# Last norm of a sparse-attention and expert layer: two tiles scaled by ScalarE and weighted by GpSimd, one expert choice summed by VectorE

## What is computed

```
proj = x @ W_in                      # q, k, v, indexer, pooling channels
mix  = concat(sparse attention with the top 128 keys, multi-scale pooling) @ W_out
h    = LayerNorm(alpha * x + mix) * ln1_g + ln1_b
# 4 groups x 8 experts; top-1 group, then top-2 experts c = 0, 1 in it, weights w[t, c]
ffn  = sum_c w[t, c] * (silu(h @ w_gate[e_c]) * (h @ w_up[e_c])) @ w_down[e_c]
out  = LayerNorm(alpha * h + ffn) * ln2_g + ln2_b
```

## Time and profile before

| | |
|---|---|
| median of 3 runs | 545.08 us (544.93 to 546.55) |
| the profiled execution | 548.01 us, its span 546.3 us |
| PE busy | 473.6 us, 87% |
| DVE busy | 227.7 us, 42% |
| ACT busy | 148.7 us, 27% |
| POOL busy | 170.3 us, 31% |
| DMA | 148.04 MB, mean 271 GB/s |
| granted TensorE clock, mean | 0.93 |

### The profile page before, as it was taken

The page is one execution under the profiler, slowest core; times in us unless marked ns, Lnnn a source line. Parts: engine busy times, 40 slices in busy tenths (PEclk is TensorE's granted clock), DMA queues, the critical chain, the costliest instruction groups (busy, mean ns, idle before and its releaser), DMA issues.

```text
span 546.3 us, 6192 instructions
## 1 busy us (share of the span) xinstructions
PE 473.6 (87%) x2210; PEld 274.2 (50%) x2210; DVE 227.7 (42%) x561; ACT 148.7 (27%) x313; POOL 170.3 (31%) x159
## 2 busy tenths in 40 slices
PE   4999999999988998996659999999877789757992
PEld 3587867687744566885624333343333333322341
DVE  2101899999856653538811112121101110101297
ACT  3323433361484673213401111021011110011032
POOL 3153599883354860333420111111111110100000
PEclk9999999999996999998559999899888998979898
DMA  9944469004088004984977999999999999999813
GB/s 313 356 61 51 51 91 390 20 1 154 1 281 297 0 1 125 427 334 175 363 260 304 398 421 421 418 420 421 419 418 422 420 421 418 422 420 386 328 54 154
DMA packets 42440, 148.04 MB, mean 271 GB/s; under 512 B 11284, under 2 KB 15892, under 8 KB 30120
## 3 DMA queue, kind: packets, MB, share of 16 engines
q1 hardware_dynamic: 37992, 139.71, 67.9%
q0 software_dynamic: 4320, 7.82, 3.9%
q10 hardware_dynamic: 96, 0.08, 0.0%
HBM read 137.16 MB, written 18.35 MB: 285 GB/s over the span
## 4 chain that ended last, share of the span: by engine, by line
PE 31%; DVE 25%; DMA 20%; SPq 15%; issue 4%; ACT 3%; POOL 2%; DVEq 0%; ACTq 0%; POOLq 0%
DMA wgu<-in_w_up_dram 10%; PE bank L1499 10%; SPq L497 10%; PE bank L1305 7%; DVE score L946 6%; DVE m L945 5%; DMA xe<-h_rows,row_from 5%; SPq L500 5%; DMA x_again<-in_x_dram 4%; DVE score L963 4%; PE bank L1523 3%; PE bank L1485 2%; PE bank L1348 2%; PE bank L1379 1%; PE bank L1587 1%
## 5 line engine op out<-in xcount | busy, mean ns | idle before, releaser
L1499 PE MATMUL bank<-wgu,xeT 128*64 128x512 f32 x512 | 128.8, 661 | 28.0 <-DMA wgu<-in_w_up_dram 27.1
L1499 PEld LDWEIGHTS bank<-wgu,xeT 128*64 128x64 f32 x512 | 42.9, 151 | 103.5 <-issue 102.4
L1128 DVE TENSOR_TENSOR act_row<-bank,sil 128x256 f32<-128x256 f32 x16 | 6.8, 424 | 152.9 <-ACT sil L857 152.9
L713 POOL DMA_INDIRECT y_rows<-ye,row_to x14 | 14.1, 1008 | 177.9 <-PE bank L1485 117.5
L1523 PE MATMUL bank<-wd,actT 128*64 128x512 f32 x256 | 57.9, 593 | 0.7 <-ACT actT L864 0.7
L620 POOL TENSOR_TENSOR ring_low<-ring,wt_high 128x1024 fp32r<-128x1024 f32 x16 | 38.7, 2416 | 42.9 <-ACT wt_high L740 42.2
L857 ACT ACTIVATE sil<-bank 128x256 f32<-128x256 f32 x16 | 6.1, 383 | 153.7 <-PE bank L1499 153.7
L1523 PEld LDWEIGHTS bank<-wd,actT 128*64 128x64 f32 x256 | 19.7, 137 | 35.6 <-issue 35.6
L1305 PE MATMUL bank<-xT_high,wt_high 128*128 128x512 f32 (+1 forms) x136 | 35.6, 406 | 0.0
L1305 PE MATMUL bank<-xT_low,wt_high 128*128 128x512 f32 (+1 forms) x136 | 35.2, 402 | 0.0
L678 POOL TENSOR_SCALAR lg<-lg,rinv 128x128 f32<-128x128 f32 (+3 forms) x32 | 22.2, 693 | 38.5 <-DVE rinv L1024 38.4
(11 more groups left out here) (199 smaller groups left out, 700.7 us busy)
## 6 DMA issues: line engine op xcount, KB each, us to landing
wgu<-in_w_gate_dram SPq DMA_DIRECT2D x32, 1024.0 KB, 21.7
wgu<-in_w_up_dram SPq DMA_DIRECT2D x32, 1024.0 KB, 26.6
wd<-in_w_down_dram SPq DMA_DIRECT2D x32, 1024.0 KB, 28.7
ring<-in_w_in_dram SPq DMA_DIRECT2D x5, 2048.0 KB, 17.2
wo<-in_w_out_dram SPq DMA_DIRECT2D x2, 2048.0 KB, 7.9
y_rows<-zero SPq DMA_DIRECT2D x1, 4096.0 KB, 21.4
yg<-y_rows SPq DMA_DIRECT2D x8, 512.0 KB, 8.7
bias_rows<-brow SPq DMA_DIRECT2D x1, 2560.0 KB
```

The lines of the kernel that those rows point to most:

```text
L1499: ins = pe.matmul(bank[2 + i][half_rows(n), :], xeT[i][:, k, half_rows(n)], wgu[slots[n]][:, :, k, :], start=k == 0, stop=k == KD - 1)
```

## The change

For tiles 0 and 1 (`BY_POOL = 2`) the normalised rows are made by other engines. VectorE's `shift(t)` forms the reciprocal of the deviation and -mean/std, two one-column instructions (L1247, L1248 of the changed kernel). ScalarE makes yg[t][0] = h * (1/std) - mean/std, one pass (L933). GpSimd multiplies it by g2 and adds b2, two passes (L736, L737), and SP waits for GpSimd's semaphore before the stores of these tiles. Tiles 2 and 3 are centred and finished by VectorE as before, the centring in a function of its own.

TensorE's `stored_rows(3)` takes only the first choice of tile 3 (two products in place of four, one diagonal matrix in place of two); VectorE adds the second with `add_stored(3, 1)`. VectorE's stored passes are split by choice and placed between the last sums.

```diff
@@ SP
             for t in range(NT):
-                sp.wait_ge(out_ready, t + 1)
+                if t < BY_POOL:
+                    sp.wait_ge(out_pool_ready, t + 1)
+                else:
+                    sp.wait_ge(out_ready, t - BY_POOL + 1)
                 sp.dma_start(ov[t], yg[t][1][:, :]).then_inc(out_stored, 16)
@@ GpSimd, behind its last store of rows
+            pool.wait_ge(ln2_in, 32)
+            for t in range(BY_POOL):
+                pool.wait_ge(norm2_ready, t + 1)
+                link(pool.tensor_tensor(yg[t][0][:, :], yg[t][0][:, :], g2[:, :], ALU.mult))
+                pool.tensor_tensor(yg[t][1][:, :], yg[t][0][:, :], b2[:, :], ALU.add).then_inc(out_pool_ready, 1)
@@ ScalarE, in the loop over tiles, behind the Sqrt
+                if t < BY_POOL:
+                    act.wait_ge(shift2_ready, t + 1)
+                    act.activation(yg[t][0][:, :], h[:, t, :], ACT.Identity, bias=row_sum[:, t, 0:1], scale=rstd2[:, t:t + 1]).then_inc(norm2_ready, 1)
@@ VectorE
-                    for c in range(2):
-                        ins = dve.tensor_scalar(by_weight[:, c, :], ident[:, :], wt[:, NT - 1, c:c + 1], None, ALU.mult)
-                    ins.then_inc(by_weight_ready, 1)
+                    dve.tensor_scalar(by_weight[:, :], ident[:, :], wt[:, NT - 1, 0:1], None, ALU.mult).then_inc(by_weight_ready, 1)
...
+            def shift(t):
+
+                dve.wait_ge(std2_ready, t + 1)
+                link(dve.reciprocal(rstd2[:, t:t + 1], std2[:, t:t + 1]))
+                dve.tensor_scalar(row_sum[:, t, 0:1], neg_mean[:, t:t + 1], rstd2[:, t:t + 1], None, ALU.mult).then_inc(shift2_ready, 1)
...
             gated(LAST)
-            add_stored(0)
-            add_stored(1)
+            for t in range(2):
+                for c in range(2):
+                    add_stored(t, c)
             y_out(LAST)
-            add_stored(2)
+            add_stored(2, 0)
+            add_last(0)
+            add_stored(2, 1)
+            add_last(1)
+            shift(0)
             dve.wait_ge(ln2_in, 32)
-            add_last(0)
-            for t in range(1, NT):
-                add_last(t)
-                finish(t - 1)
-            finish(NT - 1)
+            add_last(2)
+            centre(2)
+            shift(1)
+            add_stored(3, 1)
+            add_last(3)
+            centre(3)
+            finish(2)
+            finish(3)
@@ TensorE, stored_rows
-                    for c in range(2):
-                        pe.matmul(bank[LAST_BANKS[t][i]][:, :], by_weight[:, c, :], yg[t][c][:, 512 * i:512 * i + 512], start=c == 0, stop=False)
+                    pe.matmul(bank[LAST_BANKS[t][i]][:, :], by_weight[:, :], yg[t][0][:, 512 * i:512 * i + 512], start=True, stop=False)
```

More of the change, by code:

```diff
@@ L64 @@
 PLACE = 4
+BY_POOL = 2
 PAIR_SLOTS = ((2, 3), (1, 0), (4, 5))
@@ L176, in layer_kernel @@
         place_w = at("place_w", o + 10 * KB, [NT, 2, CAP])
-        by_weight = at("by_weight", o + 10 * KB, [2, P])
+        by_weight = at("by_weight", o + 10 * KB, [P])
         sil = [at(f"sil{i}", o + 4 * KB + KB * i, [DE]) for i in range(2)]
@@ L333, in layer_kernel @@
         std2_ready = sem("std2_ready")
+        shift2_ready = sem("shift2_ready")
+        norm2_ready = sem("norm2_ready")
+        out_pool_ready = sem("out_pool_ready")
         h_ready = sem("h_ready")
@@ L1210, in _, with add_stored @@
                         ins.then_inc(o_added, 1)
-            def add_stored(t):
+            def add_stored(t, c):
                 dve.wait_ge(y_gathered[t], 32)
-                for c in range(2):
-                    link(dve.scalar_tensor_tensor(out=h[:, t, :], in0=yg[t][c][:, :], scalar=wt[:, t, c:c + 1], in1=h[:, t, :],
-                                                  op0=ALU.mult, op1=ALU.add))
+                link(dve.scalar_tensor_tensor(out=h[:, t, :], in0=yg[t][c][:, :], scalar=wt[:, t, c:c + 1], in1=h[:, t, :],
+                                              op0=ALU.mult, op1=ALU.add))
             def add_last(t):
@@ L1225, in add_last, with centre @@
                 dve.sem_inc(mean_ready, 1)
+            def centre(t):
                 link(dve.scalar_tensor_tensor(out=yg[t][0][:, :], in0=h[:, t, :], scalar=neg_mean[:, t:t + 1], in1=g2[:, :],
                                               op0=ALU.add, op1=ALU.mult))
+            def shift(t):
+                dve.wait_ge(std2_ready, t + 1)
+                link(dve.reciprocal(rstd2[:, t:t + 1], std2[:, t:t + 1]))
+                dve.tensor_scalar(row_sum[:, t, 0:1], neg_mean[:, t:t + 1], rstd2[:, t:t + 1], None, ALU.mult).then_inc(shift2_ready, 1)
             def finish(t):
```

## The result

The changed kernel took 548.45 us (median of 15 runs, 546.58 to 550.49), the one before 545.45 (15 runs, 542.84 to 550.50). The medians differ by 3.0 us. The ratio is 1.0048 with a 95% interval of 1.0026 to 1.0070, which is slower by 2.6 us, with 1.4 to 3.8 inside the interval. The forecast was 2.5 slower, 547.6 us.

What follows compares the result with a forecast made beforehand. VectorE's last pass plus 3.1 us was taken to set the end; passes alternating with GpSimd's, 14.99 us from 530.73, end it 2.49 us later: 545.08 + 2.5 = 547.6 us. Forecast's own range 546.6 to 549; stated range 545.3 to 549.0.

Steps and rivals of the forecast that it cites:

- VectorE sets the end, the last pass plus 3.1 us: Tail: VectorE has no gap longer than about 0.1 us; the end is its last pass plus 3.1 us.
- GpSimd starts at 530.7: Tail: GpSimd's first pass on tile 0 follows ScalarE's scaling, at 530.7 us, possibly 0.2 earlier or 1.0 later.
- Alternation: Tail behind 530.7: four GpSimd passes and VectorE's five two-input SBUF passes take turns, 14.99 us to the last finish.
- held passes: Tail: VectorE's passes waiting on GpSimd; centre of tile 2 about 3.0 us, second choice of tile 3 2.9, finish 2 3.1.
- release steps: Tail: a waiting VectorE pass ends 1.10 us after its release, a waiting GpSimd pass 2.27.
- TensorE's removed work is worth nothing by itself: Last tiles' banks: TensorE loses two products, 1.7 us less, worth nothing alone because VectorE was the later of the two.
- VectorE's removed passes: Tail: VectorE loses four passes of 1.30 us, gains one and two small scalar products; net 3.4 us less.
- A product by a pointer scalar is free beside GpSimd: Tail: VectorE's two new scalar products with a pointer operand, 0.21 us each, are not held by GpSimd.
- rival 3: Tail: tile 1's shift on VectorE also waits for GpSimd's second pass; +3.0, 548.1 us; chance 10%.
- Rival 1: Tail: engines run side by side, but stores queue at about 1.25 us each; -0.3, 544.8 us, no change; chance 15%.
- Rival 2: Tail: engines run side by side and the three stores overlap, each landing 2.6 us after issue; 543.3 us, faster; chance 7%.

Runs made afterwards that it cites:

- e3: The change, but VectorE centres and finishes all four tiles, with GpSimd and ScalarE's scaling out; 547.62 us, 1.0016 of the kernel before.
- e7: The change, but TensorE sums the second choice of tile 3 again and VectorE's pass for it is out; 546.61 us, 1.0014 of the kernel before.
- e1: The change without GpSimd's four passes over tiles 0 and 1, eight columns cleared in their place; 543.13 us, 0.9944 of the kernel before.
- e2: The change with GpSimd's two passes per tile replaced by five memsets that read nothing; 546.98 us, 1.0002 of the kernel before.
- e4: The change, but ScalarE copies g2 and b2 into emptied banks, where VectorE's centre and finish read them; 546.03 us, 0.9990 of the kernel before.
- e6: As e4, but SP stores the tiles in the order 0, 2, 3, 1; 544.70 us, 0.9972 of the kernel before.

## Why the prediction was right

The mechanism was right, and so was its size. That 2.5 and 2.6 us agree to 0.1 is partly luck: the interval is far wider, and the small errors below have both signs.

1. *VectorE sets the end, the last pass plus 3.1 us.* The change ends 3.20 behind its last pass (546.1 - 542.90), e3 3.08, before 3.07. So of the 2.46 us that the tail grew, 2.33 are the last pass, where 2.49 were forecast.
2. *GpSimd starts at 530.7*, which is 24.2 us behind the first gate/up product; it was 24.37. The first sum came at 17.43 against 17.23: counted back from the end of 16 records the first bank came out 0.2 us too early. The second sum, which waits for its own bank, was 0.09 late (18.29 against 18.20), and about as much again was lost between ScalarE's end and GpSimd's start, 0.15 us (528.08 to 528.23) where the forecast had less than 0.1.
3. *Alternation.* Forecast of the held passes: 3.0, 2.9, 1.5, 3.1 us; measured 3.12, 2.93, 1.43, 3.05. The release steps were set at 1.10 and 2.27 and are 1.08 and 2.21, so the sum from GpSimd's start to the last finish was 14.67 us against 14.99. That more than cancels the late start: last finish forecast at 39.2, measured 39.04.
4. *TensorE's removed work is worth nothing by itself.* e3 and e7 show it: the 1.7 us of TensorE came with a pass of VectorE that costs 0.95 in the change and 1.74 without GpSimd. VectorE's removed passes are worth 2.83 us to its last finish where GpSimd doesn't hold the rest (e1, 36.71 - 33.88); in the change the holds took more than that.
5. *A product by a pointer scalar is free beside GpSimd* (against rival 3): L1248 of tile 1, issued at 531.89 while GpSimd's pass ran from 531.66 to 533.87, took 0.21. The prediction took rival 3 for the rule of the Trainium skill (SBUF — State Buffer, Who interferes with whom). That section says only that a tensor_scalar can enter a two-port mode, when its operands meet conditions; it doesn't say that a product over one column does, and this one was not held.
6. Rival 1 was nearly right in size where its premise is made true: without exclusion VectorE ends 2.8 us earlier than before (e1) and the queue of stores takes that back (e2, e4). From GpSimd's last pass to the end of the span e4 took 40.43 - 34.77 = 5.66 us, against 3.07 behind VectorE's last pass before, where one store is left: 1.3 us for each of the two stores more, where the rival had 1.25. Rival 2's unqueued stores did not occur.

That the second engine to come waits for the whole of the other's pass is shown by the chain of ends and by e1, e2 and e4. Which part of the memory's ports it is, no run here can tell.

## What to carry to other kernels

Work moved from VectorE to GpSimd is only off VectorE if the passes left to VectorE have at most one input in SBUF (e4), or if GpSimd's instruction reads nothing from SBUF (e2). One input on GpSimd's side is enough for exclusion, as the kernel before shows. Its L655 on GpSimd reads one tensor of SBUF, its L963 on VectorE two (timelines of before):

```profile
107.73 0.98 DVE L963 SCALAR_TENSOR_TENSOR score<-relu,iw,score 128x512 f32<-128x512 f32 x1
108.12 1.06 POOL L655 TENSOR_SCALAR_AFFINE_SELECT bias<-bias 128x512 f32<-128x512 f32 x1
108.74 0.98 DVE L963 SCALAR_TENSOR_TENSOR score<-relu,iw,score 128x512 f32<-128x512 f32 x1
...
111.79 0.75 DVE L963 SCALAR_TENSOR_TENSOR score<-relu,iw,score 128x512 f32<-128x512 f32 x1
```

The ends alternate as in the tail (108.71, 109.18, 109.72), and with GpSimd idle the same VectorE pass takes 0.75 us instead of 0.98. So count the passes with two SBUF inputs that are left to VectorE in the same stretch, and add GpSimd's to them as if both stood in one list. Where a constant operand is shared by many passes, an emptied bank takes it out of that list for one copy on an idle ScalarE. Then look at the order of the stores, since what comes ready last must not stand ahead of others in the issuing queue.

## What the runs showed of the hardware

- A VectorE pass over 1024 columns that had been issued and was waiting ended 1.08 us after GpSimd's pass, not 1.28: 0.2 us of its start lay in the wait. For GpSimd it was 2.21 against 2.35.
- With both engines always waiting they took turns one instruction each, also where GpSimd's next pass had been issued before its last one ended (533.83 against 533.87).
- ScalarE copies 1024 columns from SBUF to a bank in 1.01 us (e4), and VectorE reads the second input from there at the pace of SBUF, 1.28 us.
- The same kernel's runs spread over more than 7 us, nearly three times the effect, and ten runs gave intervals of 0.3%. Tails repeat far better: with the records' start taken to 16.16, the last finish of the four kernels in which nothing holds VectorE for long (e1, e2, e4, e6) came at 33.88, 33.87, 33.86 and 33.87 us, one profiled execution each.
